# A two-layer encoder trunk on one core: the later adaLN weight tiles asked for by GpSimd instead of SyncE

## The reference, cut to what matters

```python
def adaln(c, w, b):
    mod = (c @ w + b)[:, None, :]
    shift, scale, gate = jnp.split(mod, 3, axis=-1)
    return shift, scale, gate

for l in range(DEPTH):
    shift, scale, gate = adaln(c, w_ada_mix[l], b_ada_mix[l])
    u = x * (1.0 + scale) + shift
    y = hybrid_mixer(u, w_in[l], conv_w[l], ..., w_out[l], cos, sin)
    x = layer_norm(DN_ALPHA * x + (1.0 + gate) * y, ln1_g[l], ln1_b[l])
    shift, scale, gate = adaln(c, w_ada_ffn[l], b_ada_ffn[l])
    u = x * (1.0 + scale) + shift
    y = conv_gated_mlp(u, w_up[l], ffn_conv_w[l], ffn_conv_b[l], w_down[l])
    x = layer_norm(DN_ALPHA * x + (1.0 + gate) * y, ln2_g[l], ln2_b[l])
```

## Time and profile before

| | |
|---|---|
| median of 3 runs | 2151.9 us (2150.28 to 2152.97) |
| the profiled execution | 2151.96 us |
| its span, first to last instruction | 2150.2 us |
| granted TensorE clock, mean of the span | 0.992 of full |
| TensorE busy | 2098.3 us |
| GpSimd busy | 1406.9 us |
| VectorE busy | 1174.3 us |
| ScalarE busy | 1035.5 us |

### The profile page before, as it was taken

One profiled execution on the slowest core, in us unless ns is written; L12 is line 12 of the kernel. 1 busy time (PEld: TensorE's weight loads), 2 busy tenths in 40 slices (PEclk: granted clock), 3 DMA queues, 4 the chain that ended last, 5 costly groups with the idle time before them and its releaser, 6 DMA issues.

```text
span 2150.2 us, 27095 instructions
## 1 busy us (share of the span) xinstructions
PE 2098.3 (98%) x9499; PEld 1708.8 (79%) x9499; DVE 1174.3 (55%) x1898; ACT 1035.5 (48%) x1872; POOL 1406.9 (65%) x1769
## 2 busy tenths in 40 slices
PE   6999999999999999999999999999999999999996
PEld 5787778787888788888788888888778888888885
DVE  5698878675414454877532545587641444233224
ACT  3575356554515675364633656234552464333332
POOL 5987767765678787875557885564546776545453
PEclk9999999999999999999999999999999999999998
DMA  7644544533433354553233332332323232434332
GB/s 265 172 128 151 153 130 143 154 108 92 127 116 117 100 157 135 146 160 96 74 93 108 108 108 86 101 103 70 97 73 105 86 101 82 125 99 127 91 94 70
DMA packets 422164, 250.05 MB, mean 116 GB/s; under 512 B 49061, under 2 KB 393997, under 8 KB 422029
## 3 DMA queue, kind: packets, MB, share of 16 engines
q1 hardware_dynamic: 421162, 248.03, 38.8%
q10 hardware_dynamic: 867, 0.29, 0.1%
HBM read 242.71 MB, written 4.26 MB: 115 GB/s over the span
## 4 chain that ended last, share of the span: by engine, by line
PE 86%; POOL 5%; DVE 3%; ACT 3%; issue 1%; DMA 1%; SPq 0%; DVEq 0%; ACTq 0%; POOLq 0%
PE fg L802 27%; PE fg L804 27%; PE fg L803 27%; POOL w_lo L1717 3%; PE bank_s L880 1%; POOL ada_acc L1788 1%; DVE first_acc L1318 1%; ACT ada L1172 1%; PE bank_t L902 1%; DMA stage_in<-in_x_dram 1%; PE bank_t L889 1%; PE bank_l L819 1%; PE bank_l L912 0%; PE bank_l L814 0%; PE bank_l L824 0%
## 5 line engine op out<-in xcount | busy, mean ns | idle before, releaser
L1717 POOL TENSOR_TENSOR w_lo<-raw,w_hi 128x256 fp32r<-128x256 f32 (+1 forms) x1440 | 1041.7, 755 | 676.8 <-ACT w_hi L1022 675.9
L802 PE MATMUL fg<-u_hi,w_hi 128*128 128x512 f32 x2112 | 844.7, 400 | 10.5 <-POOL w_lo L1717 4.4
L804 PE MATMUL fg<-u_hi,w_lo 128*128 128x512 f32 x2112 | 826.3, 391 | 0.0
L803 PE MATMUL fg<-u_lo,w_hi 128*128 128x512 f32 x2112 | 826.0, 391 | 0.0
L1022 ACT ACTIVATE w_hi<-raw 128x1024 fp32r<-128x1024 f32 (+2 forms) x392 | 379.4, 968 | 423.8 <-PE fg L804 351.4
L802 PEld LDWEIGHTS fg<-u_hi,w_hi 128*128 128x128 f32 x2112 | 398.8, 189 | 109.6 <-issue 20.6
L803 PEld LDWEIGHTS fg<-u_lo,w_hi 128*128 128x128 f32 x2112 | 399.2, 189 | 85.5 <-issue 5.4
L804 PEld LDWEIGHTS fg<-u_hi,w_lo 128*128 128x128 f32 x2112 | 398.8, 189 | 85.2
L1639 DVE SCALAR_TENSOR_TENSOR x<-fg,mod,x 128x512 f32<-128x512 f32 x160 | 119.9, 749 | 353.1 <-PE fg L804 353.0
L1388 DVE SCALAR_TENSOR_TENSOR bank_c<-glu,par,bank_c 128x512 f32<-128x512 f32 x448 | 305.9, 748 | 0.1
L802 PE MATMUL fg<-h_hi,w_hi 128*128 128x512 f32 x704 | 279.5, 397 | 0.0
(11 more groups left out here) (240 smaller groups left out, 1776.4 us busy)
## 6 DMA issues: line engine op xcount, KB each, us to landing
raw<-in_w_up_dram SPq DMA_DIRECT2D x176, 512.0 KB, 3.8
ada<-in_w_ada_ffn_dram SPq DMA_DIRECT2D x48, 512.0 KB, 4.6
raw<-in_w_down_dram SPq DMA_DIRECT2D x64, 384.0 KB, 3.4
raw<-in_w_in_dram SPq DMA_DIRECT2D x40, 512.0 KB, 3.9
raw<-in_w_down_dram SPq DMA_DIRECT2D x64, 320.0 KB, 3.1
ada<-in_w_ada_mix_dram SPq DMA_DIRECT2D x32, 512.0 KB, 4.5
raw<-in_w_in_dram SPq DMA_DIRECT2D x32, 256.0 KB, 3.8
raw<-in_w_out_dram SPq DMA_DIRECT2D x32, 256.0 KB, 2.8
```

What stands on the lines that cost most here:

```text
L802: pe.matmul(out[:], hi[:, k, :], rhi, start=k == order[0], stop=False)
L803: pe.matmul(out[:], hi[:, k, :], rlo, start=False, stop=False)
L804: ins = pe.matmul(out[:], lo[:, k, :], rhi, start=False, stop=k == order[-1])
L1717: ins = pool.tensor_tensor(w_lo[n % NRAW][:, ks, :], raw[n % NRAW][:, ks, :], w_hi[n % NHI][:, ks, :].bitcast(F32), ALU.subtract)
```

## The change

The function that loads a part moves from SyncE to GpSimd. Part 0 is asked for behind `split_lo(2)`. From then on part m+1 is asked for in the slot of part m, in front of that part's additions where GpSimd makes them, and at the same place of the slot where VectorE makes them. The wait for the additions of part m-1 moves with it. SyncE keeps all other transfers, and loses the 80 of this kind with their waits. Buffers, semaphores and sizes stay. Line numbers behind L642 are lower in the changed file: L1717 becomes L1703, L1772 becomes L1758, and L1784, L1788, L1797, L1832 and L1844 stay.

```diff
             for t in range(TB, TT):
                 load_x(t)
-            load_ada(0)
             for n in range(NSLAB):
                 if n + NRAW < NSLAB:
                     sp.wait_ge(slab_done, n + 1)
                     load_w(n + NRAW)
                 for step in STEPS[n]:
-                    if step[0] == "ad":
-                        m = (step[1] - CHUNKS_BEFORE) * QUARTERS + step[2] + 1
-                        if m < QUARTERS * (4 * NCHUNK - CHUNKS_BEFORE):
-                            load_ada(m)
-                    elif step[0] == "cst":
+                    if step[0] == "cst":
                         load_cs(*step[1:])
...
+            def load_ada(m):
+
+                c, part = CHUNKS_BEFORE + m // QUARTERS, m % QUARTERS
+                l, ffn, j = c // NCHUNK // 2, c // NCHUNK % 2, c % NCHUNK
+                if m >= 2:
+                    pool.wait_ge(ada_add[added(m - 2)[0]], added(m - 2)[1])
+                src = a["w_ada_ffn" if ffn else "w_ada_mix"][l, part * 2 * P:(part + 1) * 2 * P, j * T:(j + 1) * T]
+                pool.dma_start(ada[m % 2][:], src.rearrange("(k p) n -> p k n", p=P)).then_inc(in_ada[m % 2], 16)
+
+            def next_ada(c, part):
+                m = (c - CHUNKS_BEFORE) * QUARTERS + part + 1
+                if m < QUARTERS * (4 * NCHUNK - CHUNKS_BEFORE):
+                    load_ada(m)
...
             split_lo(2)
+            load_ada(0)
             for n in range(NSLAB):
...
-                    elif what == "ad" and step[1] not in DVE_CHUNKS:
-                        add_ada(*step[1:])
+                    elif what == "ad":
+                        next_ada(*step[1:])
+                        if step[1] not in DVE_CHUNKS:
+                            add_ada(*step[1:])
```

More of the change, by code:

```diff
@@ L640, in load_first @@
                              a["w_ada_mix"][0, k0 * P:k1 * P, c0:c1].rearrange("(k p) n -> p k n", p=P)).then_inc(in_first[k], 16)
[L642 to L649, removed]
             def load_rows(rows2, rows3):
```

## The result

The changed kernel takes 2203.7 us (median of 4 runs, 2198.9 to 2204.6), against 2151.1 us for the kernel before in the same session: ratio 1.024, 95% interval 1.0227 to 1.0252, 52.6 us slower. Two slow executions further on, one of the kernel before beside the first four experiments (2338.05 us) and one of e15_vector_chunks_broken (7452.73 us), are left out of every median and difference. The prediction said slower, and 2170 us: the direction holds, the size does not, and the time lies outside the range of 2157 to 2192.

A forecast was written before the change was run, and what follows sets the result against it. TensorE was taken as the bound, busy 2098.3 of 2150.2 us. Terms (a) to (h) summed to 18.1 us on the profiled 2151.96 us, giving 2170 us, with a range of 2157 to 2192 us.

The forecast's parts named there:

- (h): Clock: a 3.3 us wait brings TensorE a stretch at the lower level, 1.2 GHz, costing 1.7 us.
- (g): All other runs of slots: `w_lo` stays 6 to 9 us ahead of its matmul, so 0 us.
- (a): Slots 1 to 4: issues and ScalarE's waits put GpSimd back before the first scores, 1.0 us.
- (f): Slots 127 to 131: five GpSimd issues, 5.5 us, against 3.0 us of slack at slab 135's low part: 2.0 us.
- (c): Slots 24 to 30, VectorE's parts: late part before slab 28, then GpSimd's slot longer than TensorE's, together 3.6 us.
- (e): Slots 48 to 51, short slabs: four issues and waiting additions against 3.6 us of slack at slab 55: 1.6 us.
- Issue 1.1 us, landing 4.5 us: Each moved load takes GpSimd 1.1 us to issue and lands 4.5 us after the issue's start.
- cheap rival: A GpSimd issue takes 0.4 us, as on SyncE; 6.8 us slower, 2159 us, chance 0.17.
- dear issue: A GpSimd issue takes about 2 us because VectorE keeps it out; 2189 us, chance 0.17.
- (b): Slots 11, 13 and 21: parts land late for ScalarE and TensorE waits, together 6.7 us.
- (d): Slots 36 to 38: two or three issues delay slab 41's low part, 1.5 us.
- Not slower: Loads land within 2.4 us of a short GpSimd issue, most waits vanish; 2151 us, chance 0.10.

The follow-up runs named there:

- e15_vector_chunks_broken: e9_only_vector_chunks, with each GpSimd low-half piece in slots 22 to 38 waiting for the end of the one before: 2167.3 us, ratio 1.0079.
- e9_only_vector_chunks: Against the kernel before, only parts 17 to 28 load through GpSimd's queue at its place, the others through SyncE's: 2164.3 us, ratio 1.0060.
- e13_spare_only_22_38: Kernel before plus GpSimd's small spare loads, which nobody reads, only in slots 22 to 38, 12 issues: 2162.1 us, ratio 1.0054.
- e8_sums_two_later: Changed kernel with the column sums of chunks 12 to 18 two slots later: 2198.4 us, ratio 1.0218 against the kernel before.
- e3_spare_issue: Kernel before plus 79 small GpSimd loads into a tile nobody reads, issued where the changed kernel asks for parts: 2173.5 us, ratio 1.0104.
- e4_late_and_spare: e1_late_on_sync plus the 79 spare GpSimd loads of e3_spare_issue: 2201.4 us, ratio 1.0233 against the kernel before.
- e1_late_on_sync: Against the kernel before, SyncE still loads the parts, but only after GpSimd's work that precedes the changed kernel's request: 2195.9 us, ratio 1.0207.
- e14_spare_twice: Kernel before with two spare GpSimd loads in place of each one of e3_spare_issue: 2263.7 us, ratio 1.0525.
- e6_sync_early: Kernel before, but SyncE asks for the next part at the slot's start, ahead of its slab wait and weight load: 2159.7 us, ratio 1.0042.

## Why the prediction was wrong, step by step

The direction was right, and in the main the places up to slot 51 and at slots 127 to 131. The term that was mis-sized most is (h), the clock: 1.7 us against 17.0, which is 15.3 of the 33 us that the sum lacks. The next is (g), taken as 0 against 7.5 us without the clock. Terms (a) to (f) together are 10.2 us short without it, and (c) and (e) had part of the mechanism wrong.

- **Issue 1.1 us, landing 4.5 us.** Measured 0.72 and 4.4 us. The landing is right; the issue lies between my value and the cheap rival's 0.4 us, so that by my own sums the time should have come out between 2159 and 2170 us. The dear issue (2 us, VectorE keeping it out) is not seen: the longest of 80 is 0.96 us.
- **(a), (b), slots 1 to 21.** 7.7 us against 9.3 measured. The waits came where they were put: TensorE stands 4.1 us ahead of the scores that come at 132.85 us in the changed kernel. Where ScalarE is the late engine the walk from slot to slot worked.
- **(c), slots 24 to 30.** 3.6 us against 11.5, of it 5.1 by the clock, the widest miss of one place. I charged the lag once (2.2 us) and then only the excess of GpSimd's slot over TensorE's (1.4 us). But here VectorE is full too (22.4 of 23.5 us), so what it waits for parts (20.3 us in the changed kernel, 13.4 in e9_only_vector_chunks) can't be made good. And the prediction has no word of an addition that GpSimd holds: 12 issues alone, with the parts in time, cost 11.9 us (e13_spare_only_22_38), 9.0 us of it seen as longer additions. VectorE and not GpSimd was late at slab 28. The last paragraph names this as a sign of error, against term (c) itself, which lets VectorE be late there.
- **(d), slots 36 to 38.** 1.5 us against 6.6, with a 5.2 us stop of TensorE from 331 us on, in which VectorE is busy throughout, 4.65 us of it with one held addition (the profile names no releaser); 6.1 us in e9_only_vector_chunks, so it is made there.
- **(e), (f), slots 48 to 51 and 127 to 131.** 1.6 and 2.0 us against 8.1 and 6.4. I measured the slack at `w_lo` of slabs 55 and 135. The first to wait was the column sum, which follows the additions by two slots and stands in no row of the prediction: 4.9 us at 413 us. e8_sums_two_later shows that to move it wins at most some 5 us, so overlooking the sum is the smaller half of this error. The greater half is GpSimd's load: the issues of a run and its waits for ScalarE add up where nothing covers them (chain of e3_spare_issue).
- **(g), the other runs.** 0 against 9.2 us, 1.7 of it clock. The slack of 6 to 9 us was read at `w_lo`; TensorE's longest stop in slabs 56 to 119, 2.0 us until 603.67, is at the line of the column sums (L898), with VectorE's `conv` as its releaser by the profile. e4_late_and_spare, which copies lateness and issue, loses 10 us less than the changed kernel from slab 56 on, so that the cause of (g)'s failure is open for the most part.
- **(h), the clock.** 1.7 us against 17.0 over the stretches, and 17.4 in TensorE's busy time. This is the largest single error. In the changed kernel TensorE stopped nine times between 65 and 2100 us for 1.9 to 5.2 us, and with each stop came a stretch at half the clock, which began during the stop or up to 3.0 us behind it, nine of them, 44.4 us together; the kernel before had two (6.8 us), and the earlier trace rows is one of them. Two of the nine (window, length, busy us and instructions of PE, PEld, DVE, ACT and POOL, granted clock, DMA share, GB/s), first the stop, then what follows:

```profile
330.80:336.40 5.60, 0.40 (x2) 0.03 (x1) 5.56 (x4) 0.00 (x0) 4.72 (x7) 0.88 0.34 96
336.50:341.00 4.50, 4.50 (x11) 3.53 (x12) 4.39 (x7) 1.30 (x2) 0.26 (x1) 0.50 0.46 127
413.20:418.40 5.20, 0.37 (x2) 0.00 (x0) 2.79 (x4) 3.01 (x4) 4.48 (x6) 0.86 0.75 241
418.50:423.00 4.50, 4.50 (x15) 3.92 (x16) 0.00 (x0) 0.17 (x1) 4.50 (x7) 0.50 0.02 6
```

The granted clock in the second and fourth is 0.50, the lower level of 1.2 GHz. I had counted one wait of 3.3 us and left out that other waits would pile up into stops of this size. The earlier trace rows has a stop of 2.0 us with such a stretch, so that by my own row a wait of 2 us, of which the sum has three more, should have been charged. For every 2 us of new idle time TensorE's busy time grew by about 1 (33.6 and 17.4 us).

- **Rivals.** Not slower: a time 2.4 us to landing was needed, it was 4.4. Cheap issue: nearer the truth for the issue, false for the result: 79 issues of 0.72 us with all parts in time cost 22.8 us (e3_spare_issue), and 12 of them 11.9 us in one stretch.

The error that (c) to (f) share is, as I read it, that I asked of each slot "how much later than its slack?", for lateness and issue time apart, and let neighbouring slack repay the rest. Where two or three engines are full at once nothing is repaid.

What the runs say of slabs 24 to 41: in 24 to 33 lateness alone (e1_late_on_sync, 9.4 us) and the issue alone (e3_spare_issue, 8.7; e13_spare_only_22_38, 9.3) each give nearly the 11.5 us of both, so either would do. In 34 to 41 the issue alone gives 0.8 us in both of its runs, against 6.6: there the late part is needed. What stays open: whether the issue's price in 24 to 33 is VectorE's held additions, and what makes the 10 us behind slab 56 that lateness and issue together don't give.

## What to carry to other kernels

Before an instruction, even a DMA issue of 0.7 us, is put on an engine, look at the busy time of all engines in the very windows where it goes: GpSimd's 65% over the span was 99% there. A load tied to an engine's own place in the program inherits that engine's lag; ask for it from an engine that isn't late, behind the transfers that are needed sooner. Price new idle time of TensorE at half as much again for the clock, as it was here. When two half experiments add up to the change's total, compare them by stretch before calling the cause found. And before blaming the long instruction on the chain, take its length away: if its engine then waits instead, it was not the cause.

## What the runs showed of the hardware

- **A short VectorE operation can be held for a whole run of GpSimd operations.** Additions with two inputs of 128x512 took 0.74 us alone, mostly 1.1 us and up to 2.8 when they began inside GpSimd's work. In all traces nine began 0.03 to 0.14 us ahead of an unbroken run of four or five GpSimd operations: they took 3.35 to 4.66 us, and eight of them ended 0.55 us behind the run's end (2.89 and 4.10 us from their start in the changed kernel). Of four that began 0.03 to 0.09 us behind a run's start one was held so (4.54 us), three took 1.3 to 1.8. With a semaphore wait between GpSimd's pieces the longest was 1.65 us. The Trainium skill ("SBUF — State Buffer", section "Who interferes with whom") says that a VectorE instruction with two inputs in the on-chip memory SBUF contends with a GpSimd instruction that reads it; the trace agrees, and shows more: not one instruction but a run of four or five was waited out.
- **Issuing on GpSimd's software queue** took 0.72 us for a part of 512 KB and as much, 0.72 us, for 64 bytes of each of its rows: the price here is that of the rows, or fixed, not that of the bytes. Of two issues directly behind each other the second began 1.7 to 4.0 us late in 26 of 79 pairs (e14_spare_twice); nothing in the profile says why.
- **A request put ahead of the weights can be slower**: on SyncE it cost 9.0 us, with the weight loads going out 1.8 us later on the mean behind its wait (e6_sync_early).
